# Conditioning products of a two-block kernel: rows scaled and summed on VectorE in three feed-forward layers, six products placed in the mixing branches, a first weight block in halves

## The reference, cut to what matters

```python
mod_l = silu(c)     @ ada_w[i] + ada_b[i]     # ada_w[i]: 1024 x 6144, i = 0, 1
mod_c = silu(c_ctx) @ ada_w[i] + ada_b[i]
```

## Time and profile before

| what | value |
| --- | --- |
| median of three executions | 3062.11 us |
| profiled execution: its own time, its span | 3060.89 us, 3059.1 us |
| TensorE (PE) busy | 2968.8 us, 97% of the span |
| VectorE (DVE) busy | 1722.9 us, 56% |
| ScalarE (ACT) busy | 711.4 us, 23% |
| DMA over the span | 142 GB/s mean |
| conditioning products from `f_ada` on TensorE | 20 x 64 records, 39.1 us busy |

### The profile page before, as it was taken

How to read it: one execution, slowest core, us unless ns; L and a number is a source line. 1 busy time by engine, 2 the same in 40 slices (tenths; PEclk the granted TensorE clock), 3 DMA queues, 4 the chain that set the end, 5 groups by cost and what they waited for, 6 DMA issues and landing times. The chain is left out here.

```text
span 3059.1 us, 53383 instructions
## 1 busy us (share of the span) xinstructions
PE 2968.8 (97%) x23066; PEld 2370.0 (77%) x23066; DVE 1722.9 (56%) x2550; ACT 711.4 (23%) x1363; POOL 83.9 (3%) x117
## 2 busy tenths in 40 slices
PE   8999999999999999999999999989999999999998
PEld 8988775559987998685558985655888887766897
DVE  5555456446557564464546566584333664486666
ACT  2102113222113101223322104282111012254210
POOL 1000000000001000000100000000000000001000
PEclk9999999999999999999999999999999999999999
DMA  8655403237656756322326744102222443331553
GB/s 290 222 178 179 149 31 111 98 110 233 206 185 197 254 174 210 124 79 95 114 84 225 247 139 152 72 1 97 83 83 83 151 153 123 106 115 56 179 166 110
DMA packets 280874, 433.13 MB, mean 142 GB/s; under 512 B 10313, under 2 KB 148065, under 8 KB 280641
## 3 DMA queue, kind: packets, MB, share of 16 engines
q1 hardware_dynamic: 273936, 411.52, 39.6%
q0 software_dynamic: 6080, 17.01, 1.6%
q10 hardware_dynamic: 624, 1.19, 0.1%
HBM read 428.62 MB, written 1.07 MB: 140 GB/s over the span
## 5 line engine op out<-in xcount | busy, mean ns | idle before, releaser
L456 PE MATMUL bank<-arena 64*64 64x64 f32 (+8 forms) x7292 | 741.5, 281 | 22.3 <-DVE arena L2065 4.6
L456 PEld LDWEIGHTS bank<-arena 128*128 128x128 f32 (+3 forms) x7292 | 641.0, 162 | 119.4 <-issue 37.1
L456 PE MATMUL bank<-xT,ring 128*128 128x128 f32 (+2 forms) x4512 | 724.2, 319 | 9.4 <-DVE arena L848 5.7
L456 PEld LDWEIGHTS bank<-xT,ring 128*128 128x128 f32 (+1 forms) x4512 | 657.3, 191 | 68.6 <-issue 9.6
L456 PE MATMUL bank<-ring,xT 128*128 128x512 f32 (+3 forms) x1648 | 577.8, 520 | 2.2 <-DVEq L2082 1.2
L456 PEld LDWEIGHTS bank<-ring,xT 128*128 128x128 f32 (+1 forms) x1648 | 264.3, 182 | 253.6 <-issue 237.1
L456 PE MATMUL bank<-ring,arena 128*128 128x256 f32 (+1 forms) x1584 | 437.0, 427 | 12.4 <-issue 5.3
L456 PEld LDWEIGHTS bank<-ring,arena 128*128 128x128 f32 x1584 | 298.2, 190 | 123.9 <-issue 82.0
L848 DVE TENSOR_TENSOR arena<-arena,bank 128x256 f32<-128x256 f32 (+1 forms) x198 | 92.2, 466 | 392.2 <-PE bank L456 250.0
L759 ACT COPY arena<-bank 128x256 f32<-128x256 f32 (+1 forms) x264 | 107.8, 408 | 746.1 <-PE bank L456 744.5
L808 DVE TENSOR_TENSOR arena<-ring,arena 128x1024 f32<-128x1024 f32 (+1 forms) x216 | 257.1, 1190 | 7.4
(11 more groups left out here) (422 smaller groups left out, 2153.6 us busy)
## 6 DMA issues: line engine op xcount, KB each, us to landing
ring<-in_ffn_w SPq DMA_DIRECT2D x88, 1024.0 KB, 8.0
ring<-in_w_in SPq DMA_DIRECT2D x32, 2048.0 KB, 7.7
ring<-in_ffn_w_in SPq DMA_DIRECT2D x44, 1024.0 KB, 7.6
arena<-in_ada_w SPq DMA_DIRECT2D x20, 2048.0 KB, 13.3
ring<-in_ffn_w SPq DMA_DIRECT2D x16, 2048.0 KB, 7.7
ring<-in_ffn_w_out SPq DMA_DIRECT2D x12, 2048.0 KB, 7.8
ring<-in_hgrn_w_in SPq DMA_DIRECT2D x12, 2048.0 KB, 7.9
ring<-in_ffn_w SPq DMA_DIRECT2D x8, 1536.0 KB, 6.7
```

The costliest lines, as they stand in the source:

```text
L456: return self.e.matmul(o, lhsT, rhs, start=start, stop=stop, skip_group_check=True)
```

## The change

It does six things.

1. **Scaled rows.** In f = 1, 2 and 3 VectorE multiplies row tiles of a conditioning product's weights by a column of `c_wide` and adds them up (`dve_ada`), for both conditions in f = 1 and 2 and for one in f = 3. Of the three products of a layer 4, 6 and 4 of the 8 row tiles go this way in f = 1 and 2, all 8 in f = 3. TensorE multiplies what is left and then adds the sums over partitions with `pick`, 4 matmuls for a condition. These steps stand at three places of blocks 2 to 8 of `dve_ffn7`: 2, 1 and 1 of them (in f = 3 only the first 2 in blocks 4 and 5).
2. **Fewer products in the layers**: 4, 3, 3, 3 instead of 5, 4, 5, 5, at blocks 3, 5, 7, 9 and 4, 7, 9.
3. **Six products in the mixing layers**, three in each: in the GLA branch after the turn of tile 0, in the delta net after the start of the solve and before its second token tile. Their weights come at home to `mix_ada`.
4. **Loads at home in three groups** of row tiles, with a semaphore each, spread over blocks 3 to 9.
5. **Start**: the first block comes in four loads, row tiles 0 to 3 first; T1 is made before the sums of x, and `first_product(0)` waits for the first half alone. TensorE multiplies 19 times zeros by zeros before the turn of x.
6. Four semaphores are dropped in favour of others that count on.

```diff
             def second_product(b):
                 if b:
                     pe.wait_ge(combined, 4 * (up_before(f) + b - 1) + 3)
+                elif f == 0:
+                    pe.wait_ge(block_landed[0], pe.landed[0])
...
@@ dve_ffn7, block b
                 combine(0, w.s[:, 0], single[:, 0:w.T])
                 dve_T(dve, f, b + 1)
+                pieces = ADA_PIECES[f].get(b, (0, 0, 0))
+                dve_ada(dve, pieces[0])
                 dve.wait_ge(products, product_count(f, b, 6))
                 dve.wait_ge(products_kept, 4 * n + 3)
                 combine(2, w.s[:, 2], pair[:, 0:w.T])
+                dve_ada(dve, pieces[1])
                 dve.wait_ge(products_kept, 4 * n + 4)
                 combine(1, w.s[:, 3], single[:, 0:w.T])
                 combine(3, w.s[:, 3], w.s[:, 1])
...
                 if b >= 4 and (w.streams == 1 or b < 8):
                     hidden_sum(0, b // 4 - 1, b % 4)
+                dve_ada(dve, pieces[2])
...
-        IN_FFN = (((3, 5, 7, 8, 9), (3, 5, 7, 9)), ((3, 5, 7, 8, 9), (3, 5, 7, 8, 9)))
+        IN_FFN = (((3, 5, 7, 9), (4, 7, 9)), ((4, 7, 9), (4, 7, 9)))
+        IN_MIX = 3
...
+        ADA_GROUPS = ((0, 2), (2, 4), (4, 8))
+        ADA_SCALED = (0,) * 4 + (0,) * IN_MIX + (4, 6, 4) + (0,) + (4, 6, 4) + (0,) * IN_MIX + (8, 8, 8)
...
+        FULL = {b: (2, 1, 1) for b in range(2, 9)}
+        ADA_PIECES = ({}, FULL, FULL, {**FULL, 4: (2, 0, 0), 5: (2, 0, 0)}, {}, {})
...
+        def dve_ada(dve, n):
...
+                if k:
+                    ins = v.scalar_tensor_tensor(sums, f_ada[:, k], scale, sums, ALU.mult, ALU.add)
+                else:
+                    dve.wait_ge(ada_used, i)
+                    ins = v.tensor_scalar(sums, f_ada[:, k], scale, None, ALU.mult)
+                ins.then_inc(dve_step, dve.up(dve_step))
+                dve.wait_ge(dve_step, dve.sent(dve_step))
+                if s == ada_streams(i)[-1] and k in ada_signals(ADA_SCALED[i]):
+                    dve.sem_inc(ada_scaled, dve.up(ada_scaled))
...
@@ pe_ada_product
-            for k in range(KT):
+            for k in range(scaled, KT):
...
+            if scaled:
+                pe.wait_ge(ada_scaled, ada_scaled_due(i, scaled - 1))
+                streams = ada_streams(i)
+                for s in streams:
+                    for j in range(4):
+                        mm = pe.mm(bank[32 * j:32 * j + 32, 0:P], pick[:, 31 - s:63 - s],
+                                   f_ada_sum[:, s, j * P:(j + 1) * P], s == 0 and scaled == KT, s == streams[-1])
...
@@ pe_mix and act_gla, pe_gdn and act_gdn
-            pe_branch(pe)
+            pe_branch(pe, turned=lambda: pe_ada_product(pe, mix_ada))
...
             act_branch_turned(act, 0, cols[:, GLAG:GLAG + 1])
+            act_ada_product(act, True)
             act_prepare_sqrt(act)
...
+            act_ada_turn(act)
+            act_ada_product(act, True)
             act_solve(act, dPm)
...
             for tt in range(2):
+                if tt:
+                    modulation()
                 pe.wait_ge(to_act.freed, to_act.next_free())
...
@@ SyncE, mixing layer
+                    if n == 1:
+                        eng.wait_ge(branch_ready, 6 * l + 2)
+                    if n:
+                        modulation_at_home(mix_ada)
...
@@ start
+            pe.wait_ge(xT_dve_ready, pe.due(xT_dve_ready))
+            for _ in range(WAKE):
+                pe.mm(psum[0][:, 0:P], zeros, zeros)
             pe.wait_ge(ident_landed, pe.due(ident_landed, 16))
...
+                if l == 0:
+                    dve_T(dve, 0, 0, range(1))
                 dve_x_sums(dve)
                 if l == 0:
-                    dve_T(dve, 0, 0)
+                    dve_T(dve, 0, 0, range(1, 4))
```

More of the change, by code:

```diff
@@ L144, in two_blocks @@
         ada_used = sem("ada_used")
-        ada_landed = sem("ada_landed")
+        ada_landed = [sem(f"ada_landed{g}") for g in range(3)]
+        ada_scaled = sem("ada_scaled")
         ada_rows_ready = sem("ada_rows_ready")
@@ L486, in used @@
                 self.to_release += 1
+        WAKE = 19
+        zeros = xT[:, KT - 1, SEQ:SEQ + P]
         def pe_program(eng):
@@ new lines, in two_blocks @@
+        IN_MIX = 3
+        ADA_KINDS = [kind for l in range(DEPTH) for kind in
+                     ["home"] * len(IN_FFN[l][0]) + ["ring"] * IN_TRANSITION[l][0] + ["home"] * IN_MIX
+                     + ["ring"] * IN_TRANSITION[l][1] + ["home"] * (len(IN_FFN[l][1]) + IN_TRANSITION[l][2])
+                     + ["ring"] * IN_TRANSITION[l][3]]
+        ADA_HOME = [m for m, kind in enumerate(ADA_KINDS) if kind == "home"]
+        ADA_RING = [m for m, kind in enumerate(ADA_KINDS) if kind == "ring"]
@@ new lines, in two_blocks, with ada_streams, ada_signals, ada_scaled_due @@
+        ADA_PIECES = ({}, FULL, FULL, {**FULL, 4: (2, 0, 0), 5: (2, 0, 0)}, {}, {})
+        def ada_streams(i):
+            return (0, 1) if ADA_HOME[i] < 16 else (0,)
+        def ada_signals(nk):
+            return [k for k in range(nk) if k in (1, 3) or k > 3 and k == nk - 1]
+        def ada_scaled_due(i, k):
+            return sum(len(ada_signals(n)) for n in ADA_SCALED[:i]) + len([x for x in ada_signals(ADA_SCALED[i]) if x <= k])
+        ADA_STEPS = [(i, k, s) for i, n in enumerate(ADA_SCALED) for k in range(n) for s in ada_streams(i)]
@@ new lines, in two_blocks @@
+        assert len(ADA_STEPS) == sum(sum(x) for f in ADA_PIECES for x in f.values())
+        def dve_ada(dve, n):
+            v = nc.vector
+            for _ in range(n):
+                i, k, s = ADA_STEPS[dve.ada]
+                dve.ada += 1
+                sums, scale = f_ada_sum[:, s], c_wide[:, k, s:s + 1]
+                if s == 0 and k in (0, 2, 4):
+                    dve.wait_ge(ada_landed[k // 2], 16 * (i + 1))
+                if k:
+                    ins = v.scalar_tensor_tensor(sums, f_ada[:, k], scale, sums, ALU.mult, ALU.add)
+                else:
+                    dve.wait_ge(ada_used, i)
+                    ins = v.tensor_scalar(sums, f_ada[:, k], scale, None, ALU.mult)
+                ins.then_inc(dve_step, dve.up(dve_step))
+                dve.wait_ge(dve_step, dve.sent(dve_step))
+                if s == ada_streams(i)[-1] and k in ada_signals(ADA_SCALED[i]):
+                    dve.sem_inc(ada_scaled, dve.up(ada_scaled))
@@ new lines, in two_blocks, with pe_ada_product @@
+        assert all(n % 2 == 0 or not m for t in IN_TRANSITION for n, m in enumerate(t))
+        assert sum(sum(n) for n in IN_TRANSITION) + sum(len(m) for n in IN_FFN for m in n) + DEPTH * IN_MIX == ADA_BLOCKS
+        def pe_ada_product(pe, home=None):
+            scaled = 0
+            if home is not None:
+                i = pe.homes
+                pe.homes += 1
+                scaled = ADA_SCALED[i]
+                for g, (_, k1) in enumerate(ADA_GROUPS):
+                    if k1 > scaled:
+                        pe.wait_ge(ada_landed[g], 16 * (i + 1))
+                blk = home
@@ L4620, in first_pe @@
                 last = l == DEPTH - 1
[L4621 removed]
+                ada = [ffn_ada(marks, lambda: pe_ada_product(pe, f_ada), lambda: pe_ada_turn(pe)) for marks in IN_FFN[l]]
                 if l == 0:
```

139 lines of the change are left out of this document (86 added, 53 removed).

## The result

The changed kernel took 3076.82 us, the median of 4 runs (3075.88 to 3080.58), beside 3061.71 us of the kernel before on the same chip. The ratio is 1.0052, with a 95% interval of 1.0040 to 1.0064: slower by half a per cent, 15.1 us. The forecast was 3067.0, no change with a lean to slower; its range, 3054 to 3078, holds the time, and of its rivals it is the clock that came. The times of the kernels are medians, and they leave out one execution of the sums in time (4459 us) and one of the late constants (3253 us), whose mean granted clock was 0.64 and 0.91 (the expectations give the first of these two as 3049.6 us, with that execution in).

What follows compares the result with a forecast made beforehand. TensorE, with matmuls in flight for 97% of the span, was taken as the bound. Terms -13.1 + 5.2 - 0.7 + 14.4 - 2.6 + 1.7 = +4.9 us on 3062.1 gave 3067.0 us, range 3054 to 3078.

Steps and rivals of the forecast that it cites:

- the clock: Rival, slower: TensorE's clock drops after five to seven long waits, costing 8.5 to 11.9 us, 3073.8 to 3077.2; chance 0.30.
- part 5: TensorE's new waits for the scaled-row sums: one drop to half clock, +1.7 us, bounds 0 and 11.9.
- Six products leave, -13.1: Feed-forward layers: 19 conditioning products become 13, each saving 2.18 us with its turn, 13.1 us in all.
- Scaled rows, +14.4: Nine products in f = 1 to 3: 22.2 us of TensorE waits for VectorE's sums against 7.8 us of matmuls saved.
- Mixing layers, +5.2 - 0.7: Six products moved there delay 2.6 us a layer, 5.2 in two; 0.7 gained from clock kept up in layer 1.
- The new loads are hidden: Mixing layers: 2 MB loads take some 13.3 us, each asked for one product ahead, tens of microseconds before use; no cost.
- The 0.7 for the fall in layer 1: Second token tile of mixing layer 1: a product in the 1.76 us wait probably keeps the clock up, gaining 0.7 us.
- The start, -2.6: Program start: split first block, zero multiplications and an earlier weight sum save 2.6 us, bounds 1.0 and 3.4.
- The chain of block 0: Start: 11.1 + 2.9 + 3.8 = 17.8 us, combination done at 18.3, product at 18.4 to 19.1 instead of 21.24.
- The rival of the sums in time: Faster: last step comes before the block's end, no waits or clock drop, 3043.1 us; chance 0.14, including much cheaper waits.
- The rival of full price in the mixing layers: Slower: products moved there cost 13.1 us in place of 5.2, 3074.9 us; chance 0.10, shared with no gain at start.
- that of nothing gained at the start: Rival: first half lands as late as the whole block did, +2.6, 3069.6 us; chance 0.10, shared with full mixing-layer price.

Runs made afterwards that it cites:

- sums in time: Changed kernel with the fourth scaled-row step of each block moved ahead of the last two combinations; 3048.89 us, ratio 0.9962.
- late constants: Kernel with the sums in time, plus POOL's two loads of constants asked for only after block 1's weights landed; 3046.97 us, ratio 0.9957.
- filled waits: Changed kernel with identity multiplications on TensorE ahead of the nine waits for the sums, computing other modulations; 3067.40 us, ratio 1.0021.
- late load: Kernel with the sums in time, plus each mixing layer's third load of conditioning rows held until the solve has ended; 3047.95 us, ratio 0.9956.
- sums later: Changed kernel with one more scaled-row step of each block moved behind the last two combinations; 3091.56 us, ratio 1.0102.

## Why the prediction came out as it did

The step that failed is part 5, the clock: "I take one fall, 1.7". There were five, and each cost 1.6 us: 8.1 in place of 1.7. The price of a fall and the upper bound were right, the number was not. I weighed the form of the work (wide matmuls) against the length of the waits on two rows, one with a fall and one without, and took the milder reading. It is the rival with five to seven falls that happened. That its 3073.8 to 3077.2 hold the time is in part luck: with five falls of 1.6 us the forecast's other terms give 3073.4, and what is missing came from the mixing layers (3.3 us) and the start (1.9), less 1.5 elsewhere. That the range holds the time owes it to the rivals it was drawn for: the forecast alone, 3061 to 3070, doesn't, and its sum was 10 us short. The rule of the Trainium skill that I set beside it ("TensorE: Matmul & The Clock Gate", section "HAM oscillation — how this bites in real kernels"), that a long enough wait between bursts sends the clock back and the next burst starts slow, agrees in kind with the five stretches, behind waits of 2.06 to 3.16 us, while four of the nine waits, up to 2.50 us, had no fall behind them.

Term by term:

- *Six products leave, -13.1.* Right: 2.19 in f = 0 and 2.19, 4.38 and 4.37 in the run without scaled rows, 13.1 in all.
- *Scaled rows, +14.4.* Right in mechanism and nearly in size: filled waits against no scaled rows give 407.11 - 393.46 = 13.7 us. The place of the last step, the wait it makes and its length all came as worked out (20.5 us of waits, 22.2 forecast; TensorE's own 16 matmuls took 1.08 and not 0.84). Moving that one step changed the time by 28 us.
- *Mixing layers, +5.2 - 0.7.* Too small by 3.3: measured 3.06 + 4.79 = 7.85. The first branch cost 1.23 (1.2 forecast), the second token tile 0.3 (0.25), the last turn nothing (0.2). The start of the solve cost 1.21 against 0.9, and behind it came pauses of 1.05 and 1.26 us that I had no term for. "The new loads are hidden" is the step that failed: they are hidden as data, but the third one is in flight over a stretch of small matmuls, and the late load takes those pauses out. Up to the last turn of RWKV the first layer got 1.1 us shorter and the second 1.3 longer; there the pauses come and go from kernel to kernel, and they too end as a packet of instructions has landed. The 0.7 for the fall in layer 1 came, and by its size: from the second token tile to the last `w_branch` 15.14 us where it was 15.81. But the kernel with the start alone took 15.13 there, without a product in the wait and without a fall, so the gain can't be put down to the product.
- *The start, -2.6.* Measured -0.70 in the changed kernel, -1.2 alone. The chain of block 0 was right within 0.3 us (the combination done at 18.13, 18.3 forecast; the product at 18.18, 18.4 to 19.1 forecast). What I left out is the next block: its weights landed at 21.70, and the DMA engines moved some 350 GB/s from 3 us on. With 640 KB out of their way the same edit gave 2.4.
- *The rest of the program*, after the last `keep(3)` of f = 3, got 0.76 us shorter, and 0.5 to 0.9 in the other kernels with products in the mixing layers, but for the sums later, which had a stretch at 0.5 there and got 0.7 longer; it had no term, and its cause wasn't looked for.

In sum -0.7 - 13.1 + 7.9 + 13.7 + 8.1 - 0.8 = +15.1 us; the spans differ by 15.0.

The rival of the sums in time gave 3043.1 for this kernel if the last step came before the end of the block. That did not happen in the change as made, but the idle time that it needs was there, one step further forward in each block: the run with the step moved took 3048.9, and 3043.1 with the mixing layers and the start as they turned out (3.3 and 1.9 us) is 3048.3. The rival of full price in the mixing layers is ruled out by the 3.06 and 4.79 us for three products each, against 6.5; that of nothing gained at the start is nearly what happened, by another way than the one named.

## What to carry to other kernels

Work put on an idle engine is free only if its last piece stands before the point where the busy engine needs it: look not at how much idle time there is but at what the last piece is queued behind, and one place forward can be worth more than the work itself. A wait of the bounding engine can cost the slower clock behind it besides its length: the nine here, of 1.3 to 3.2 us, cost 20.5 us and 8.1 us of clock. A large load beside a stretch of small matmuls can hold up the engine's own instructions. And when the start of a program is made quicker, ask first what lands next and what shares its way.

## What the hardware showed that was not expected

- Clock falls are not a matter of the length of the wait alone: 2.06 us was followed by one twice and 2.49 and 2.50 us were not, 2.12 us twice not; every wait of 2.85 us or more was, in both kernels that had them. One and the same wait of 1.76 us was followed by a fall in the kernel before and by none with the start alone. Each of the five stretches of the changed kernel lasted 3.4 us and cost 1.6 us. What decides is open. Stretches of the same kind came in the first mixing layer in three of the ten kernels profiled (389.0, 390.5 and 411.0 us), well ahead of the products put there.
- TensorE can stand still for 0.2 to 1.6 us in stretches of small matmuls with nothing to wait for that the profile shows. All 74 such pauses end 1.2 to 1.6 us after 16 KB of instructions have landed, and in the solve they went when a load of 2 MB no longer ran beside it.
- The scaled step with its factor read from a tile took 0.752 us over 65 instructions, as the nearest row said (0.751).
